# Three changes of order at the transitions of a transformer-block kernel: the fourth unit's low part, the freeing of the banks, three splits

## The reference

```python
# first block (mLSTM)
h = h + 0.5 * rmsnorm(swiglu(rmsnorm(h, gn[0]), ffn_w_in[0], ffn_w_out[0]), gn[1])   # FFN 0
h = h + rmsnorm(mlstm_mixer(rmsnorm(h, gn[2]), ...), gn[3])
h = h + 0.5 * rmsnorm(swiglu(rmsnorm(h, gn[4]), ffn_w_in[1], ffn_w_out[1]), gn[5])   # FFN 1
# second block (latent attention and retention)
h = h + 0.5 * swiglu_2(rms_norm(h, ffn1_norm), ...)                                  # FFN 2
h = h + concat(mla_group(...), retention_group(...)) @ w_o
h = h + 0.5 * swiglu_2(rms_norm(h, ffn2_norm), ...)                                  # FFN 3
return rms_norm(h, final_norm)
```

## Time and profile before

| what | value |
|---|---|
| median of three runs | 2025.77 us |
| the profiled execution's own time | 2020.28 us |
| its span, first to last instruction | 2018.1 us |
| PE busy | 1954.6 us (97% of the span) |
| DVE, ACT, POOL busy | 1231.7, 945.8, 925.7 us |
| mean granted TensorE clock | 0.994 |
| PE's share of the chain that ended last | 85%; DVE 8%, ACT 3%, POOL 1% |

### The profile page before, as it was taken

The page is one execution under the profiler, slowest core; times in us unless marked ns, Lnnn a source line. Parts: engine busy times, 40 slices in busy tenths (PEclk is TensorE's granted clock), DMA queues, the critical chain, the costliest instruction groups (busy, mean ns, idle before and its releaser), DMA issues.

```text
span 2018.1 us, 35966 instructions
## 1 busy us (share of the span) xinstructions
PE 1954.6 (97%) x13132; PEld 1746.8 (87%) x13132; DVE 1231.7 (61%) x1705; ACT 945.8 (47%) x1628; POOL 925.7 (46%) x535
## 2 busy tenths in 40 slices
PE   7999999999999899999989999999999999999998
PEld 7999999987788799988878999887775678999887
DVE  6876660384355887781288778315856537777711
ACT  4566642334324566662255666324436435666521
POOL 4354464533315455564454555544441034555552
PEclk9999999999999999999999999999999999999999
DMA  5233333322213133333322333334311022333331
GB/s 162 64 104 104 102 106 97 84 54 83 66 43 94 53 105 104 104 114 98 92 63 85 107 110 107 107 89 108 82 50 43 12 79 68 108 109 105 105 105 52
DMA packets 343054, 177.87 MB, mean 88 GB/s; under 512 B 18715, under 2 KB 338070, under 8 KB 342958
## 3 DMA queue, kind: packets, MB, share of 16 engines
q1 hardware_dynamic: 341104, 175.46, 30.4%
q10 hardware_dynamic: 1854, 1.07, 0.2%
HBM read 174.42 MB, written 2.10 MB: 87 GB/s over the span
## 4 chain that ended last, share of the span: by engine, by line
PE 85%; DVE 8%; ACT 3%; issue 2%; POOL 1%; DMA 0%; SPq 0%; DVEq 0%; ACTq 0%
PE ps L2266 43%; PE ps L2508 35%; DVE hid_r L1502 1%; DVE E L1720 1%; DVE xop L1418 1%; PE ps L3005 1%; POOL wlo L471 1%; PE ps L2987 1%; PE ps L2964 1%; PE ps L2340 1%; POOL hT L488 1%; DVE xlo L1666 1%; DMA raw<-in_ffn_w_in 0%; DVE xop_f L1392 0%; PE ps L2296 0%
## 5 line engine op out<-in xcount | busy, mean ns | idle before, releaser
L471 POOL TENSOR_TENSOR wlo<-raw,whi 128x1024 fp32r<-128x1024 f32 x192 | 487.2, 2548 | 638.8 <-ACT whi L591 638.2
L2508 PE MATMUL ps<-xop,whi 128*128 128x256 f32 (+1 forms) x4032 | 723.6, 282 | 15.6 <-DVE wlo L1460 6.7
L2508 PEld LDWEIGHTS ps<-xop,whi 128*128 128x128 f32 x4032 | 620.9, 189 | 18.4 <-issue 10.2
L2508 PE MATMUL ps<-xop,wlo 128*128 128x256 f32 (+1 forms) x2016 | 567.1, 281 | 0.0
L528 POOL TENSOR_TENSOR wlo<-raw,whi 128x512 fp32r<-128x512 f32 x212 | 289.3, 1369 | 216.7 <-ACT whi L668 216.6
L2508 PEld LDWEIGHTS ps<-xop,wlo 128*128 128x128 f32 x2016 | 381.9, 189 | 0.0
L2266 PE MATMUL ps<-xop,whi 128*128 128x512 f32 (+3 forms) x1148 | 331.7, 346 | 2.0 <-DVE hid_r L1502 2.0
L2266 PE MATMUL ps<-xop,wlo 128*128 128x512 f32 (+3 forms) x902 | 287.6, 347 | 0.0
L591 ACT ACTIVATE whi<-raw 128x1024 fp32r<-128x1024 f32 x176 | 183.1, 1052 | 202.5 <-PE ps L2266 194.2
L668 ACT ACTIVATE whi<-stage 128x512 fp32r<-128x512 f32 x216 | 136.4, 631 | 210.9 <-DVE stage L1442 132.8
L2266 PEld LDWEIGHTS ps<-xop,whi 128*128 128x128 f32 x1148 | 198.2, 188 | 32.6 <-DVE hid_r L1502 3.3
(11 more groups left out here) (373 smaller groups left out, 2914.1 us busy)
## 6 DMA issues: line engine op xcount, KB each, us to landing
raw<-in_ffn_w_in SPq DMA_DIRECT2D x88, 512.0 KB, 3.9
raw<-in_ffn_w_gate SPq DMA_DIRECT2D x44, 512.0 KB, 3.8
raw<-in_ffn_w_up SPq DMA_DIRECT2D x44, 512.0 KB, 3.8
raw<-in_ffn_w_out SPq DMA_DIRECT2D x32, 512.0 KB, 3.9
raw<-in_ffn_w_down SPq DMA_DIRECT2D x32, 512.0 KB, 3.8
raw<-in_a_w_in SPq DMA_DIRECT2D x24, 512.0 KB, 3.7
raw<-in_w_in SPq DMA_DIRECT2D x19, 512.0 KB, 3.9
raw<-in_ffn_w_out SPq DMA_DIRECT2D x16, 384.0 KB, 3.4
```

The source lines that it names most:

```text
L471: pool.tensor_tensor(wlo[:, u % SLOTS, :], raw[:, u % SLOTS, :], whi[:, u % SLOTS, :].bitcast(F32), ALU.subtract).then_inc(lo_done, 1)
L2508: ins = pe.matmul(ps[:, bank_, 0:h], w[l][:, k * P:(k + 1) * P], x[r][:, k * h:(k + 1) * h], start=start and k == 0 and q == 0, stop=k == ...
```

## The change

It moves instructions on four engines, and adds and removes none.

- POOL, all three transitions: the low part of u0+3 goes behind the second half's additions.
- DVE, transitions 1 and 2: `free_ffn` goes ahead of the additions of squares.
- PE, transitions 1 and 2: in unit u0+3 the sums go from ahead of k = 2 to ahead of k = 3, the spread from ahead of k = 4 to ahead of k = 5.
- ACT, transitions 1 and 2: the splits of u0+4, u0+5 and u0+6 go ahead of the root.
- ACT, all four FFNs: `hi_a11` goes ahead of silu(2), and in FFNs 1 to 3 `keep_a21` too.

```diff
@@ def pool_transition
         pool_res_half(pool, i, 0, 4, KD)
+        pool_res_half(pool, i, 1, 1, KD)
         pool_lo(pool, u_next + 3, u_next + 4)
-        pool_res_half(pool, i, 1, 1, KD)
@@ def act_ffn
         x_hi(("S2", "A22"), c_s["x_diff"], [c_at["x_diff"] + q for q in (3, 4)])
+        hi_a11((None, 0))
+        if n == SEQ:
+            keep_a21((None, 0))
         silu(2)
-
-        hi_a11((None, 0))
-        keep_a21((None, 0))
+        if n == TOK:
+            keep_a21((None, 0))
@@ def prog_scalar
         act_transition(act, 1, U_M1 + 25, 1, R1, 2, "norm_gains", 32)
-        split_to(act, FFNS[1]["u0"])
+        split_to_conv(act, FFNS[1]["u0"], 3)
         act_root(act, N2)
...
         act_transition(act, 2, FFNS[1]["u0"] + NU_UP, 3, R2, 3, "ffn1_norm_2", 0)
-        split_to(act, FFNS[2]["u0"])
+        split_to_conv(act, FFNS[2]["u0"], 3)
         act_root(act, N3)
@@ def dve_transition
+        if i > 0:
+            free_ffn(v)
         for k in range(1, KD):
             sum_square(v, norm, k, n)
@@ def prog_vector
         dve_transition(v, 1, m1["y"], U_M1 + 25, 1, (24, 1.0), R1, 2, "norm_gains", 32)
-        free_ffn(v)
         dve_rms(v, N2)
...
         dve_transition(v, 2, ybuf, FFNS[1]["u0"] + NU_UP, 3, (40, 0.5), R2, 3, "ffn1_norm_2", 0)
-        free_ffn(v)
         dve_rms(v, N3)
@@ def pe_ffn
         def halved(k):
-            if k == 2:
+            if k == 3:
                 sum_norm(pe, norm, n)
-            if k == 4:
+            if k == 5:
                 spread(pe, rms)
```

## The result

The changed kernel takes 2029.3 us (median of 20 runs, 2025.15 to 2032.19), the kernel before 2024.66 beside it. The ratio is 1.0025, with an interval of 1.0018 to 1.0033: slower by 0.25%, about 5.1 us. The forecast was 2028.0 us and 0.1%, with "within 0.2%" as the likeliest case. The time lies inside the range, on the side above 0.2%. Part of the closeness of the time is luck.

What follows compares the result with a forecast made beforehand. PE was busy 97% of the span, with DVE's chain setting the fast part's start; twice +1.4 us, less 0.7 (transition 0), plus 0.1 (FFN 0) gave +2.2, so 2025.77 became 2028.0 us, range 2017.8 to 2032.5.

Steps and rivals of the forecast that it cites:

- POOL's order: Transitions: three `xlo` take 1.5 us, not 3.63; PE's 1.18 wait goes; additions of squares gain 0.4; transition 0 gains 0.7.
- Banks and sums: Transitions 1 and 2: PE's 1.68 wait for the cell goes, sums one step later at 29.7; these edits cost nothing.
- The splits: Ahead of the root: early splits let POOL's low parts stop the sixth and seventh additions; PE's sums 2.2 us later.
- rival A: Additions of squares: only the seventh is stopped, as a back-to-back DVE instruction can slip through; 2020.6 us, chance 0.21.
- The clock: Behind each of two new PE stalls: half granted clock costs 1.5 us, bounds 0 and 1.7.
- What comes back: FFN: low parts done earlier return 2.9 us to DVE's chain; PE's 1.30 wait for u0+4 goes.
- silu(2): FFNs: hi_a11 and keep_a21 ahead of it put POOL's A11 low part between `x_lo`; 0.65 us more, 0.1 in FFN 0.
- The sum: Per transition 1 and 2: 2.2 + 1.5 - 2.9 + 0.65 = +1.4 us; +2.2 us in all.
- Rival B: Additions of squares: none is stopped, sums at 29.9, 4.2 us gained per transition; 2016.8 us, chance 0.10.
- Rival D: Transitions: PE's waits go, but DVE keeps the start of the fast part; within 1 us of before, chance 0.12.
- rival C: Additions of squares: three are stopped, or a longer clock loss behind the stall ends alike; 2032.7 us, chance 0.13.

Runs made afterwards that it cites:

- root-first kernel: The changed kernel with ACT's root ahead of the three splits again, as in the kernel before: 2022.88 us, 0.9991 times before.
- kernel in which POOL waits: The changed kernel, with POOL beginning the low part of u0+4 in FFNs 1 and 2 only when the squares are summed: 2015.42 us, 0.9953 times before; again 2016.34.
- filler: The changed kernel with 36 unread products on PE right ahead of the sums in unit u0+3 of FFNs 1 and 2: 2024.31 us, 1.0000 times before.
- both repairs: The changed kernel with POOL's u0+4 held until the squares are summed and silu(2) ahead of hi_a11 and keep_a21 again: 2012.49 us, 0.9941 times before; again 2015.28.

## Why the prediction was right, and where it was short

Its steps in order, with times of transition 2 like before, less 1000.

- **POOL's order.** Right. PE's wait of 1.18 for `xlo` is gone. The three `xlo` took 1.50 us (forecast 1.5); POOL's low part of u0+3 ran from 22.31 to 24.94 (22.4 to 24.95) and stopped the last `xlo` until 25.22 (25.25); the first addition began at 25.16 (25.2). Transition 0, from PE's wait for `xlo` to the end of its stall, became 0.62 us shorter (30.67 to 30.05); the forecast was 0.7. One premise of it was off: in the kernel before PE came to the sums of transition 0 without a wait (414.46, the additions ended at 414.18), and only in the changed one does it wait for them, 0.54 us.
- **Banks and sums.** Right. PE began u0+3 at 27.18 without a wait (27.5) and stood at the sums from 29.5 (29.7). They cost nothing, as forecast, and by themselves they bring something: the root-first kernel has them and the kernel with POOL's order alone hasn't, and PE comes to its sums 4.72 us behind the first addition in the one and 6.30 in the other (transition 2). The two differ in silu's order as well, but that stands behind the sums. In the changed kernel the collision takes this gain away again.
- **The splits.** Right: the choice on which most hung came out as taken. ACT began at 26.74 (26.97), POOL at 27.88 (28.1), and the sixth and seventh additions took 2.75 and 2.71 us. POOL's issue came 0.53 us before the sixth's, and POOL won. The Trainium skill, "SBUF — State Buffer", section "Who interferes with whom", states that the order of issue decides which of the two blocks the other; by that rule POOL wins, and the trace agrees here, though not in the earlier trace rows. What rival A made of the earlier trace rows, that a back-to-back instruction slips through, isn't the whole of it either. In the changed kernel's `x_lo` pair POOL began 0.69 us ahead of the second, which followed the first without a gap, and it was stopped all the same (2.32 us in place of 1.21); in the earlier trace rows the lead was 0.28 us and nothing was stopped. An addition that waits for its forerunner was stopped with a lead of 0.31 us as well, in the kernel with the splits alone. What decides between these cases no run shows. PE summed at 33.96 (34.15), 2.0 us later than before (2.2). The root-first kernel shows that the early splits are the cause, and the kernel in which POOL waits shows that they act through POOL's low parts and not by themselves.
- **The clock.** Here the forecast was short, and this is the term of the sum that was mis-sized. It took the loss from the earlier trace rows, 3.45 us at 0.51, as 1.5 with an upper bound of 1.7. Here the clock stood at 0.50 for 5.1 us behind the stall and for 1.6 us before its end, and the way from the sums to the scaled grew by 2.5 (3.56 to 6.06). The filler confirms 2.4 to 2.5 by itself. The bound was no bound: the earlier trace rows showed how long one stretch was in another place, and I read it as a length that belongs to every stall. The stretch had no cover either, because ACT and DVE wait for the sums and the spread.
- **What comes back.** Right: L1404's successor took 1.21 us, L1387's 1.40 (0.69 + 0.7), and the scaled block to the end of L1404 took 9.12 us in place of 12.02, the 2.9 of the forecast. PE's wait for u0+4 is gone.
- **silu(2).** Right in size: +0.73 in transition 2 (0.65). In FFN 0 it was 0.2 (0.1). The reading behind it was loose: in the kernel before, of the 2.15 us of POOL's low part only 0.68 lie beside an instruction that reads PSUM (L1384 at 1058.04); it began beside an `x_lo` pair that took its free 2.35 us all the same, and held up one L1387 by 0.4 (1.07 in place of 0.69).
- **The sum.** +2.0 + 2.5 - 2.9 + 0.73 is +2.33 us in transition 2, which is what the marks from PE's first wait of the halves to S1 show (48.65 to 50.98); +2.40 in transition 1. Twice 2.4, less 0.6, plus 0.2 is +4.3 us, 0.2%, where the forecast had 2.2. Nearly all of the difference, 2.0, is the clock's. The measured 5.1 has an interval from 3.6 to 6.7 that holds the 4.3.

One stopped addition, the count of rival A, is what the splits do alone, in the kernel before; but there POOL came too late for the sixth, and no back-to-back addition slipped through. Rival B's time, 2016.8 us for no addition stopped, came out when POOL was made to wait (2015.4 and 2016.3), with its -4.2 per transition. Rival D did not come up. Of rival C the three stopped additions did not, but its last clause did: a loss of clock that lasts longer behind the stall.

What stays open: the two profiled spans differ by 7.7 us, and the transitions account for some 4.1. The rest follows stretches of low clock elsewhere, which one execution has longer than the other. The changed kernel is 2.0 us ahead when transition 0 begins, and it loses 1.3 us behind S1 in FFN 1, 1.25 behind S1 in FFN 2, 1.2 in the attention part behind PE's wait of 3.64 us there and 1.5 just ahead of FFN 3. The last two lie where the change edits nothing, and the clock stood at 0.50 for twice as long there as in the execution of the kernel before (at least 6.7 us against some 3.4).

Whether the change makes the stretches at the starts of the fast parts longer, these profiles don't decide. Over the 20 us from 5 us behind S1 the mean granted clock in FFNs 1 / 2 is 1.00 / 0.91 in the kernel before, 0.83 / 0.83 and 0.91 / 0.83 in the two profiles of the changed one, 0.91 / 0.91 with silu's old order, 0.83 / 0.83 and 0.83 / 1.00 where POOL waits, and 0.91 / 0.91 and 0.91 / 0.83 with both repairs. They may be why the old order of silu is worth 2.4 to 3.4 us by the ratios and 1.6 by the timelines, but the intervals are wide enough that no such reason is needed.

## What to carry to other kernels

Work brought forward into an engine's idle time is free only if it stops no instruction of another engine that the critical chain needs then. Here POOL's low parts stopped DVE's additions, which read two tiles of SBUF each. Look at what the critical chain does in that time, and hold the early work behind its last result (one wait turned +0.25% into -0.4%). A stall of PE can cost more than its length, where the products behind it run at half clock; price it by how long the low stretch may last and by who waits for those products, and shorten or fill the stall if the wait can't be removed. Closing several short waits can make a long one, so add them up in the order of time and not by kind.

## What the runs showed that I had not expected

- The stretch of half clock behind a stall has no fixed length: 3.45 us in the earlier trace rows behind 4.40 us, 5.1 here behind 4.50, with 1.6 more inside the stall.
- A wait of 2.60 us brought the clock down to 0.51 in transition 1 and one of 2.62 left it in transition 2, in the same execution of the same kernel.
- How many additions POOL stops hangs on a fraction of a microsecond: begun during the fifth, its low part stopped the sixth (2.75 us in place of 0.69); begun 0.42 us behind the start of the sixth, it let that one through and stopped the seventh.
- 36 products that nobody reads, in the stall, made the kernel faster by 0.25 to 0.29% than the same kernel without them.
